# Gate and up products with tokens in the array, 512 weight columns wide, and the hidden product turned by TensorE

## The reference, cut to what matters

```python
def swiglu(h, w_gate, w_up, w_down):
    return (jax.nn.silu(h @ w_gate) * (h @ w_up)) @ w_down

x = x + 0.5 * swiglu(rmsnorm(x, norm), w_gate, w_up, w_down)   # the first has factor 1
```

## Time and profile before

| | |
|---|---|
| time, median of 3 runs | 1365.27 us (1365.24 to 1365.31) |
| profiled execution, first to last instruction (span) | 1363.5 us |
| around the span (median less span) | 1.8 us |
| TensorE busy | 1357.7 us, 7385 matmuls |
| VectorE, ScalarE, GpSimd busy | 943.0, 713.1, 151.9 us |
| HBM read | 244.45 MB |

### The profile page before, as it was taken

How to read it: one execution, slowest core, us unless ns; L and a number is a source line. 1 busy time by engine, 2 the same in 40 slices (tenths; PEclk the granted TensorE clock), 3 DMA queues, 4 the chain that set the end, 5 groups by cost and what they waited for, 6 DMA issues and landing times.

```text
span 1363.5 us, 19187 instructions
## 1 busy us (share of the span) xinstructions
PE 1357.7 (100%) x7385; PEld 1156.2 (85%) x7385; DVE 943.0 (69%) x1175; ACT 713.1 (52%) x943; POOL 151.9 (11%) x172
## 2 busy tenths in 40 slices
PE   9999999999999999999999999999999999999999
PEld 8987888888888888887788888888888887888887
DVE  6894667666677666768666666676667788676665
ACT  5566446444465444577664444544445677544442
POOL 4052003000030000042020000200000332200000
PEclk9999999999999999999999999999999999999999
DMA  9654458655546555554346655465565442555552
GB/s 272 204 165 139 170 169 286 211 194 196 192 155 211 190 185 185 177 182 136 124 155 207 194 185 185 157 213 186 190 195 189 164 155 94 178 192 187 190 197 73
DMA packets 164859, 246.34 MB, mean 181 GB/s; under 512 B 4952, under 2 KB 121860, under 8 KB 164672
## 3 DMA queue, kind: packets, MB, share of 16 engines
q1 hardware_dynamic: 162736, 240.19, 53.9%
q0 software_dynamic: 1776, 4.74, 1.2%
q10 hardware_dynamic: 288, 0.61, 0.1%
HBM read 244.45 MB, written 1.07 MB: 180 GB/s over the span
## 4 chain that ended last, share of the span: by engine, by line
PE 98%; ACT 1%; DVE 1%; issue 0%; ACTq 0%
PE ps L1672 29%; PE ps L1639 16%; PE ps L1677 15%; PE ps L1641 15%; PE ps L1640 15%; PE ps L1881 1%; PE ps L1665 1%; PE ps L1919 1%; PE ps L1935 1%; PE ps L2200 1%; PE ps L1943 0%; PE ps L1968 0%; PE ps L1974 0%; PE ps L1978 0%; PE ps L1845 0%
## 5 line engine op out<-in xcount | busy, mean ns | idle before, releaser
L1672 PE MATMUL ps<-xx,whi 128*128 128x512 f32 x1760 | 422.1, 391 | 0.0
L1672 PEld LDWEIGHTS ps<-xx,whi 128*128 128x128 f32 x1760 | 325.5, 188 | 64.5
L1007 DVE TENSOR_TENSOR wlo<-raw,whi 128x2048 fp32r<-128x2048 f32 x120 | 275.1, 2293 | 94.4 <-ACT whi L641 94.4
L641 ACT ACTIVATE whi<-raw 128x2048 fp32r<-128x2048 f32 x120 | 229.5, 1912 | 122.7 <-PE ps L1641 122.5
L633 ACT ACTIVATE whi<-raw 128x2048 fp32r<-128x2048 f32 (+1 forms) x135 | 205.2, 1531 | 75.4 <-PE ps L1641 63.5
L1677 PEld LDWEIGHTS ps<-xx,wlo 128*128 128x128 f32 x1760 | 227.6, 191 | 9.9
L1677 PE MATMUL ps<-xx,wlo 128*128 128x256 f32 x1760 | 230.6, 283 | 0.0
L1639 PE MATMUL ps<-whi,hhi 128*128 128x512 f32 x504 | 198.7, 394 | 0.0
L1640 PE MATMUL ps<-wlo,hhi 128*128 128x512 f32 x504 | 196.8, 390 | 0.0
L1641 PE MATMUL ps<-whi,hlo 128*128 128x512 f32 x504 | 196.3, 390 | 0.0
L1002 DVE TENSOR_TENSOR wlo<-raw,whi 128x2048 fp32r<-128x2048 f32 x75 | 171.5, 2288 | 32.5 <-ACT whi L633 32.4
(11 more groups left out here) (282 smaller groups left out, 1388.9 us busy)
## 6 DMA issues: line engine op xcount, KB each, us to landing
raw<-in_ffn_w_gate SPq DMA_DIRECT2D x44, 1024.0 KB, 5.3
raw<-in_ffn_w_up SPq DMA_DIRECT2D x44, 1024.0 KB, 5.3
raw<-in_ffn_w_down SPq DMA_DIRECT2D x44, 1024.0 KB, 4.9
raw<-in_w_in SPq DMA_DIRECT2D x40, 1024.0 KB, 5.1
raw<-in_w_gate_up SPq DMA_DIRECT2D x22, 1024.0 KB, 5.1
raw<-in_w_out SPq DMA_DIRECT2D x12, 1024.0 KB, 4.9
raw<-in_w_down SPq DMA_DIRECT2D x11, 1024.0 KB, 5.0
raw<-in_w_mem_kv SPq DMA_DIRECT2D x4, 1024.0 KB, 5.1
```

What stands on the lines that cost most here:

```text
L641: act.activation(whi[:, c % 3, :], raw[:, c % 3, :], ACT.Copy).then_inc(hi_done, 1)
L1007: dve.tensor_tensor(wlo[:, c % 3, :], raw[:, c % 3, :], whi[:, c % 3, :], ALU.subtract)\
L1672: return pe.matmul(ps[:, bank + n, :], whi[:, slot, 256 * k + P * n:256 * k + P * n + P], both, start=start, stop=False)
```

## The change

The gate and up weights are laid out in DRAM so that a step's 256 gate and 256 up columns stand side by side, and a unit is now 4 chunks x 512 columns (two units, or halves, per step, where it was gate and up). In TensorE stand 128 tokens (hi, then lo), and the 512 columns stream past them: three matmuls of 512 per chunk and block of tokens. So gate and up of a block of 128 tokens lie in the two halves of one bank, tokens on partitions. ScalarE takes SiLU out of PSUM with the token's factor as its scale, one block at a time (`silu`, with the new signal `first_tile` for block 0), VectorE multiplies by up out of PSUM (`hidden`), and the product, tokens on partitions, is turned by TensorE, four transposes (`turn_hidden`), into one bank. ScalarE copies hi from there (`hidden_hi`), VectorE subtracts lo (`hidden_lo`). The two crosswise copies, the two additions, the scaling pass and the spreading of the factors go.

The turn of step J lies behind the first 6 matmuls of the down unit that follows gate and up of J, and for step 0 between the hi and the lo matmuls of the third unit. The first two units of a feed-forward (`first_half`) wait for `lo_done` of their unit and go chunk by chunk with all three matmuls.

```diff
-            def against_both(bank, slot, n, k, start):
-                both = xx[:, k, :, :].rearrange("p a b -> p (a b)")
-                return pe.matmul(ps[:, bank + n, :], whi[:, slot, 256 * k + P * n:256 * k + P * n + P], both,
-                                 start=start, stop=False)
-            def against_first(bank, slot, n, k, stop):
-                return pe.matmul(ps[:, bank + n, 0:SEQ], wlo[:, slot, 256 * k + P * n:256 * k + P * n + P], xhi[:, k, :],
-                                 start=False, stop=stop)
-            def first_unit(u, slot, T, idx):
+            def first_half(u, half, T, idx):
                 pe.wait_ge(lo_done, u + 1)
-                for k in range(0, KC, 2):
-                    if k == 2:
+                for k in range(4):
+                    if half == 0 and k == 2:
                         turn_rows(T, 1, (2, 3), 4 * idx + 4)
-                    for kk in (k, k + 1):
-                        pe.wait_ge(xlo_done, KC * T + kk + 1)
-                        for n in range(2):
-                            against_both(4, slot, n, kk, kk == 0)
-                    for kk in (k, k + 1):
-                        for n in range(2):
-                            ins = against_first(4, slot, n, kk, kk == KC - 1)
+                    pe.wait_ge(xlo_done, KC * T + 4 * half + k + 1)
+                    for r in range(RT):
+                        ins = three(ps[:, gate_banks(0)[r], :], x(4 * half + k, P * r, P), w(u % 3, 512 * k, 512),
+                                    half == 0 and k == 0, half == 1 and k == 3)
+                        if half == 1 and k == 3 and r == 0:
+                            ins.then_inc(first_tile, 1)
                 ins.then_inc(unit_used, 1)
-            def column_unit(u, slot, bank):
+            def gate_up_half(u, slot, half, banks, between=None):
                 pe.wait_ge(hi_done, u + 1)
-                for n in range(2):
-                    for k in range(KC):
-                        against_both(bank, slot, n, k, k == 0)
+                for r in range(RT):
+                    for k in range(4):
+                        for part in range(2):
+                            pe.matmul(ps[:, banks[r], :], x(4 * half + k, P * r, P)[part], whi[:, slot, 512 * k:512 * k + 512],
+                                      start=half == 0 and k == 0 and part == 0, stop=False)
+                if between:
+                    between()
                 pe.wait_ge(lo_done, u + 1)
-                for n in range(2):
-                    for k in range(KC):
-                        ins = against_first(bank, slot, n, k, k == KC - 1)
+                for r in range(RT):
+                    for k in range(4):
+                        ins = pe.matmul(ps[:, banks[r], :], x(4 * half + k, P * r, P)[0], wlo[:, slot, 512 * k:512 * k + 512],
+                                        start=False, stop=half == 1 and k == 3)
+                    if half == 1 and r == 0:
+                        ins.then_inc(first_tile, 1)
                 ins.then_inc(unit_used, 1)
-            def row_scales(f):
-                ones = cst[:, C_ONE:C_ONE + P]
-                pe.wait_ge(diag_ready, 2 * f + 2)
-                for r in range(RT):
-                    ins = pe.matmul(ps[:, 6, P * r:P * r + P], ones, rdg[:, r, :], start=True, stop=True)
-                ins.then_inc(rb_ps, 1)
+            def turn_hidden(J, bank):
+                pe.wait_ge(h_mul, J * 2 + 2)
+                for n in range(4):
+                    ins = pe.transpose(ps[:, bank, P * n:P * n + P], hid[:, P * n:P * n + P], ident)
+                ins.then_inc(h_ps, 1)
...
                 for r in range(RT):
                     for c in range(2):
+                        if between and (r, c) == (0, 1):
+                            between()
...
-                    pe.wait_ge(gate_sum, J)
-                    column_unit(u, slot, 0)
-                    pe.wait_ge(up_sum, J)
-                    column_unit(u + 1, (slot + 1) % 3, 2)
+                    pe.wait_ge(h_ready, J)
+                    gate_up_half(u, slot, 0, banks)
+                    gate_up_half(u + 1, (slot + 1) % 3, 1, banks)
...
-                first_unit(u0, u0 % 3, T, idx)
-                column_unit(u0 + 1, (u0 + 1) % 3, 2)
-                column_unit(u0 + 2, (u0 + 2) % 3, 0)
-                row_scales(f)
-                pe.wait_ge(up_sum, j0 + 1)
-                column_unit(u0 + 3, (u0 + 3) % 3, 2)
-                down_step(j0, u0 + 4, (u0 + 4) % 3, 0, first=True)
+                first_half(u0, 0, T, idx)
+                first_half(u0 + 1, 1, T, idx)
+                gate_up_half(u0 + 2, (u0 + 2) % 3, 0, gate_banks(1), lambda: turn_hidden(j0, turn_bank(0)))
+                gate_up_half(u0 + 3, (u0 + 3) % 3, 1, gate_banks(1))
+                down_step(j0, u0 + 4, (u0 + 4) % 3, 0, first=True, between=lambda: turn_hidden(j0 + 1, turn_bank(1)))
```

ScalarE and VectorE in the loop (k is 0 or 1):

```diff
-                        gate_copy(i * 2 + (j0 + 2 + k), i * 6 + (u0 + 6 + 3 * k))
+                        J = i * 2 + (j0 + 2 + k)
                         hi_at(i, u0 + 8 + 3 * k)
-                        silu(i * 2 + (j0 + 2 + k))
-                        up_copy(i * 2 + (j0 + 2 + k), i * 6 + (u0 + 7 + 3 * k))
+                        silu(J, gate_banks(2 + k), i * 6 + (u0 + 6 + 3 * k))
+                        hidden_hi(J, k, turn_bank(2 + k))
                         hi_at(i, u0 + 9 + 3 * k)
                         hi_at(i, u0 + 10 + 3 * k)
...
-                        gate_add(i * 2 + (j0 + 2 + k))
-                        gate_scaled(i * 2 + (j0 + 2 + k))
                         lo_at(i, u + 3)
-                        up_add(i * 2 + (j0 + 2 + k))
-                        hidden(i * 2 + (j0 + 2 + k))
+                        hidden(J, gate_banks(2 + k))
+                        hidden_lo(J, k, turn_bank(2 + k))
                         lo_at(i, u + 4)
-                        split(i * 2 + (j0 + 2 + k), k)
                         lo_at(i, u + 5)
```

More of the change, by code:

```diff
@@ L744, in ffn, with silu @@
-                act.wait_ge(rb_ps, f + 1)
-                act.activation(rbc, ps[:, 6, 0:SEQ], ACT.Copy).then_inc(rb_ready, 1)
-                silu(j0)
+                def silu(J, banks, u):
+                    for r in range(RT):
+                        if r == 0:
+                            act.wait_ge(first_tile, J + 1)
+                            if not isinstance(J, int) or J > 0:
+                                act.wait_ge(h_mul, J * 2)
+                            if f == 1:
+                                act.wait_ge(frs_ready, 2)
+                            else:
+                                act.wait_ge(rstd_ready, place((N_FFN, N_F1, N_F2, N_F3, N_F4)[f], RT - 1) + 1)
+                        else:
+                            act.wait_ge(unit_used, u + 1)
+                        act.activation(sil[:, SEQ * r:SEQ * r + SEQ], ps[:, banks[r], 0:SEQ], ACT.Silu,
+                                       scale=row_factor(f, r)).then_inc(silu_done, 1)
@@ L751, in ffn @@
+                hidden_hi(j0 + 1, 1, turn_bank(1))
                 hi(u0 + 6, (u0 + 6) % 3)
@@ L1195, in hidden @@
[L1195 to L1205 removed]
+                def hidden(J, banks):
+                    for r in range(RT):
+                        dve.wait_ge(silu_done, J * 2 + r + 1)
+                        if r == 0 and (not isinstance(J, int) or J > 0):
+                            dve.wait_ge(h_ps, J)
+                        v = slice(SEQ * r, SEQ * r + SEQ)
+                        dve.tensor_tensor(hid[:, v], ps[:, banks[r], SEQ:2 * SEQ], sil[:, v], ALU.mult).then_inc(h_mul, 1)
@@ L1738, in wide, with down @@
                 ins.then_inc(unit_used, 1)
-            def down(u, slot, banks, first, left):
+            def down(u, slot, banks, first, left, between=None):
                 pe.wait_ge(lo_done, u + 1)
@@ L1748, in down, with last_two @@
                 ins.then_inc(unit_used, 1)
-            def last_two(u, banks, lefts, ready, T=None, idx=None):
+            def last_two(u, banks, lefts, ready, T=None, idx=None, between=None):
                 def part(r, k, n, last):
@@ L1763, in last_two @@
                     part(r, 0, n, False)
+                    if between and (r, n) == (0, 0):
+                        between()
                 pe.wait_ge(*ready[1])
@@ L2265, with steps @@
     given["mem_t"] = np.asarray(inputs["mem_2"])[0].reshape(SEQ, KC, P).transpose(2, 1, 0)
+    def steps(gate, up):
+        both = [np.asarray(v).reshape(DM, STEPS, 1, 256) for v in (gate, up)]
+        return np.concatenate(both, 2).reshape(DM, 2 * FF)
+    gate_up = np.asarray(given.pop("w_gate_up"))[0]
+    given["gate_up"] = steps(gate_up[:, :FF], gate_up[:, FF:])
+    for n in ("ffn1", "ffn2"):
+        gate, up = given.pop(f"{n}_w_gate_2"), given.pop(f"{n}_w_up_2")
+        given[f"{n}_gate_up"] = np.stack([steps(gate[L], up[L]) for L in range(2)])
     for name, a in given.items():
```

158 lines of the change are left out of this document (52 added, 106 removed).

## The result

The changed kernel takes 1386.24 us (median; 1385.72 to 1386.54) beside 1365.29 us for the kernel before on the same chip: a ratio of 1.0151, with a 95% interval of 1.0139 to 1.0163. It is 1.5% slower, 20.9 us. The forecast was 1386.7 us. The profiled execution's span is 1384.7 us, 21.2 above the 1363.5 of before.

The account below looks back on a forecast made before the run. TensorE was taken as the bound, so only its own sequence counted: 12.9 - 2.3 + 9.1 + 0.7 + 1.0 = +21.4 us on the profiled 1363.5, plus 1.8 from span to median, gives 1386.7 us; range 1376 to 1398.

Parts of the forecast that it names:

- no rival: Three rivals: turn late in every step (0.12), start waits don't come (0.10), transposes at their columns' price (0.06).
- The step: Each of 55 feed-forward steps: four transposes +0.475 us, fewer matmuls -0.24, so +0.235 us per step, +12.9 us in all.
- the rival of transposes at their columns' price: Turns in the steps: four transposes cost only 0.264 us; no change or faster, 1364 to 1365 us; chance 0.06.
- The starts: Start of each feed-forward: TensorE waits for VectorE's lo of unit 1, 3 x 1.9 and 2 x 1.7 us, +9.1 us.
- The second feed-forward's scale: Second feed-forward's first turn: first SiLU waits for the factor from GpSimd's chain, +0.7 us (0 to 1.5).
- The turn inside a step: Behind 6 matmuls of the down unit: the product just fits; 0.02 us in 50 steps, +1 us (bounds 0 to +10).
- The row factors: Once per feed-forward: matmuls spreading the row factors go from TensorE, 5 x 0.45 = -2.3 us.

Follow-up runs that it names:

- lo_by_256: Changed kernel with each matmul of lo weights (all halves but a feed-forward's first two) cut into two of 256 columns, 800 more matmuls: 1398.42 us.
- turn_twice: Changed kernel with each turn made twice into the same place, 8 transposes per step instead of 4: 1410.81 us.
- turn_spread: Changed kernel with the turn's four transposes placed singly between matmuls of the down unit, in 47 of 55 turns: 1387.17 us.
- hi_first: Changed kernel with the second half of a feed-forward's first step running its hi matmuls before it waits for lo: 1381.06 us.
- rows_at_1: Changed kernel with the activations' last four transposes behind a feed-forward's first chunk instead of the second: 1380.26 us.
- turn_at_12: Changed kernel with the turn behind 12 instead of 6 matmuls of the down unit: 1388.82 us.
- turn_at_3: Changed kernel with the turn behind 3 instead of 6 matmuls of the down unit: 1414.77 us.

## Why the prediction was right

The mechanism and the size both held; no rival came. One term was luck, as said below.

*The step.* Forecast +0.235 us, measured 16.81 - 16.58 = +0.23. Its two halves hold too: gate and up 10.88 us (forecast 10.89), the down unit with its turn 5.93 (forecast 5.45 + 0.475 = 5.925). lo_by_256 put the fixed price of a matmul at 0.014 us and 0.0156 with what follows, rather than 0.012; as the forecast took it only as an explanation and priced the 48 matmuls at the measured 0.2269, no error came of it. turn_twice and turn_spread bore out the price of a transpose, 0.11 us in any position, and ruled out the rival of transposes at their columns' price. So 16 matmuls fewer of 64 save 0.22 us, four transposes cost 0.43 to 0.48, and the step's +0.23 times 55 is 12.7 of the 21.2 us.

*The starts.* Forecast +9.1, five waits of 1.9 us of which two save 0.3. The waits view has five of 1.7 (8.6). The forecast was worked out by starts, and by starts TensorE is 1.87 us late; with the slower first matmul behind the stand it is 1.98, five times less the same 0.3 twice: 9.3. The third feed-forward shows the saving: its transposes begin at 702.69, 2.75 behind its first matmul, without a wait. hi_first and rows_at_1 remove the waits in two ways, and show that they were real: 2.0 us come back per feed-forward where nothing else is late. Where only TensorE is freed, 4.9 us come back in all: the factor, VectorE's lo behind a slow transfer, and 1.3 us at the lower clock take the rest.

*The second feed-forward's scale.* Forecast +0.7, measured a wait of 1.0 us, 1.1 by starts. Counted from the feed-forward's first matmul the factor came 0.73 us later than before, inside the 0 to 1.3 given. What was too short is the way behind it: 1.75 us from the factor to the first transpose instead of 1.3, with one more GpSimd instruction (0.26) and both blocks of SiLU in it. The increments per feed-forward agree. The forecast for the first is 11 x 0.235 - 0.45 + 1.9 = 4.04, and 4.09 was measured; for the others it is 4.74 and 5.10, 3.84 and 3.75, 4.04 and 3.83, 3.84 and 3.67.

*The turn inside a step.* Forecast to fit by a few hundredths, with +1.0 us for steps where it wouldn't. It fits in every step but the second feed-forward's first, where the factor is late, and turn_at_12 finds no wait hidden. turn_at_3 shows how near it was: 0.68 us (3 matmuls) earlier cost 0.54 us per step, so about 0.1 us were free. The 1.0 us was too much, and the unforeseen 0.76 us at the program's start, which varies between executions, happened to fill its place; the agreement to 0.5 us is luck to that extent.

*The row factors.* Forecast -2.3, measured about -2 by doubling them in the kernel before.

## What to carry to other kernels

Where TensorE is the bound and each matmul carries its own weight load, count a matmul at its columns plus a fixed 0.012 to 0.016 us (as measured here at 256 and 512 columns): fewer, wider ones save little, and a turn of the result (0.11 us per 128x128 in float32) costs more than it frees on engines that were hidden. When the count per chunk of a start changes, look at what stands in fixed order behind it (here the last transposes, then VectorE's lo): the shift comes out as a wait in every stage. A cure that frees only the waiting engine gives part of it back at the next late thing, here an instruction that stands in fixed order ahead of the wanted one, and a longer stand there can cost the clock too; one that moved the whole chain earlier kept its gain.

## What the runs showed of the hardware

A transfer of 1 MB took 4.8 us, and 16.5 us when GpSimd's four loads had been issued before it, at a DMA share of 0.92 and 331 GB/s; issued 1.3 us earlier it landed at the same moment, and in a run with GpSimd's loads issued 2.2 us earlier it landed 2.3 us earlier. A stall of TensorE costs more than its idle time in the profile, which begins when the last matmul's passage ends: 0.50 us late against 0.35 idle at a turn, 1.87 against 1.72 at a start. The first matmul or transpose behind it costs more besides (0.34 us instead of 0.23 at a start). A load of 44 KB at the program's start took 4.3 to 6.0 us in executions of kernels with the same start. In hi_first the granted clock fell to 0.50, the 1.2 GHz level, while TensorE stood for 2.98 us, and 1.3 us were lost before it was back at 1.000. In the profiles of the changed kernel and of the other runs, with the added transposes and with stands of up to 1.8 us, the mean granted clock was 1.000, the 2.4 GHz level.
